# Down weights by output columns, both layers ending in PSUM, and 19 first places for expert weights

## The reference

```python
def grouped_moe(h, router_w, router_bias, w_gate, w_up, w_down):
    ...                                # each token: 1 of 4 groups, then the top 2 of its 4 experts
    a = jnp.einsum('td,edf->etf', t, w_gate)
    u = jnp.einsum('td,edf->etf', t, w_up)
    hidden = jax.nn.silu(a) * u * gates.T.astype(t.dtype)[..., None]
    out = jnp.einsum('etf,efd->td', hidden, w_down)
...
for l in range(DEPTH):
    mix = hybrid_mixer(x, w_in[l], attn_sinks[l], conv_w[l], a_log[l], dt_bias[l],
                       dn_norm_w[l], w_out[l], cos, sin)
    x = layer_norm(ALPHA * x + mix, ln1_g[l], ln1_b[l])
    ffn = grouped_moe(x, router_w, router_bias, w_gate[l], w_up[l], w_down[l])
    x = layer_norm(ALPHA * x + ffn, ln2_g[l], ln2_b[l])
```

## Time and profile before

| | us |
|---|---|
| median of three runs | 1999.3 |
| the profiled execution | 1998.46 |
| its span, first to last instruction | 1996.7 |
| PE busy | 1921.4 |
| DVE busy | 686.5 |
| ACT busy | 329.5 |
| DMA queue q1, share of 16 engines | 69.0% |

### The profile page before, as it was taken

How to read it: one execution, slowest core, us unless ns; L and a number is a source line. 1 busy time by engine, 2 the same in 40 slices (tenths; PEclk the granted TensorE clock), 3 DMA queues, 4 the chain that set the end, 5 groups by cost and what they waited for, 6 DMA issues and landing times.

```text
span 1996.7 us, 27957 instructions
## 1 busy us (share of the span) xinstructions
PE 1921.4 (96%) x11409; PEld 1194.3 (60%) x11409; DVE 686.5 (34%) x1385; ACT 329.5 (17%) x616; POOL 103.0 (5%) x174
## 2 busy tenths in 40 slices
PE   8999999999999999999899999999999999999996
PEld 7888886666644434444488888766665444443443
DVE  5444434553501111111483434445534011111104
ACT  1104220110311110111211231111103111110112
POOL 4000030012000000000000001200210000000000
PEclk9999999999999999999999999999999999999998
DMA  7433342228699999999934434422397999999995
GB/s 243 148 127 127 127 148 86 85 64 321 271 408 422 422 422 422 422 422 422 406 112 146 139 112 147 135 75 68 103 368 275 411 421 422 422 422 422 422 421 243
DMA packets 128842, 539.16 MB, mean 270 GB/s; under 512 B 15856, under 2 KB 20464, under 8 KB 78320
## 3 DMA queue, kind: packets, MB, share of 16 engines
q1 hardware_dynamic: 128752, 537.86, 69.0%
HBM read 535.73 MB, written 2.10 MB: 269 GB/s over the span
## 4 chain that ended last, share of the span: by engine, by line
PE 68%; DMA 25%; DVE 5%; issue 1%; ACT 0%; SPq 0%; DVEq 0%; ACTq 0%
PE bank L860 17%; DMA ring<-in_w_down_dram 13%; DMA ring<-in_w_up_dram 12%; PE bank L1405 10%; PE bank L871 9%; PE bank L919 8%; PE bank L1453 6%; PE bank L1190 3%; PE bank L953 3%; PE bank L1337 3%; PE bank L787 1%; DMA x_t<-in_w_up_dram 1%; PE bank L1066 1%; PE bank L1349 0%; PE bank L1161 0%
## 5 line engine op out<-in xcount | busy, mean ns | idle before, releaser
L860 PE MATMUL bank<-x_t,ring 128*128 128x256 f32 x1536 | 342.6, 382 | 0.0
L860 PEld LDWEIGHTS bank<-x_t,ring 128*128 128x128 f32 x1536 | 288.4, 190 | 48.8 <-issue 11.2
L2333 DVE TENSOR_TENSOR region_a<-bank,region_a 128x512 f32<-128x512 f32 x16 | 11.1, 692 | 566.3 <-PE bank L1405 566.3
L1405 PE MATMUL bank<-ring,region_a 128*64 128x512 f32 x704 | 159.6, 596 | 13.1 <-DMA ring<-in_w_up_dram 13.1
L1337 PEld LDWEIGHTS bank<-prob_t,x_nat 128*128 128x128 f32 x1024 | 115.5, 192 | 12.0 <-issue 11.4
L871 PE MATMUL bank<-ring,mix_acc 128*128 128x512 f32 x256 | 121.3, 604 | 1.4 <-ACT mix_acc L1663 1.4
L1453 PE MATMUL bank<-ring,region_a 128*64 128x512 f32 x512 | 115.1, 594 | 5.9 <-DMA ring<-in_w_down_dram 5.8
L1337 PE MATMUL bank<-prob_t,x_nat 128*128 128x128 f32 x1024 | 118.6, 277 | 0.0
L1405 PEld LDWEIGHTS bank<-ring,region_a 128*64 128x64 f32 x704 | 51.6, 137 | 109.3 <-issue 107.6
L1453 PE MATMUL bank<-region_b,region_a 128*64 128x512 f32 x384 | 113.3, 596 | 1.7 <-ACT region_a L1710 1.7
L2346 DVE SCALAR_TENSOR_TENSOR y_lo<-bank,slot_gate,y_hi 128x512 fp32r<-128x512 f32 x64 | 48.0, 750 | 193.1 <-ACT y_hi L1722 187.9
(11 more groups left out here) (424 smaller groups left out, 2413.0 us busy)
## 6 DMA issues: line engine op xcount, KB each, us to landing
ring<-in_w_up_dram SPq DMA_DIRECT2D x88, 1024.0 KB, 19.5
ring<-in_w_in_dram SPq DMA_DIRECT2D x80, 1024.0 KB, 5.0
ring<-in_w_down_dram SPq DMA_DIRECT2D x64, 1024.0 KB, 23.4
region_b<-in_w_gate_dram SPq DMA_DIRECT2D x48, 1024.0 KB, 19.6
region_b<-in_w_down_dram SPq DMA_DIRECT2D x48, 1024.0 KB, 20.6
ring<-in_w_gate_dram SPq DMA_DIRECT2D x36, 1024.0 KB, 22.4
ring<-in_w_out_dram SPq DMA_DIRECT2D x32, 1024.0 KB, 5.2
x_t<-in_w_up_dram SPq DMA_DIRECT2D x32, 1024.0 KB, 19.1
```

Of the source, the lines that this page charges most:

```text
L860: m = pe.matmul(b[c // 2][:, (c % 2) * T:(c % 2 + 1) * T], w[:, kk, c * P:(c + 1) * P], xT[:, k, :], start=(k == 0 and c % 2 == 0), stop=( ...
L1405: m = pe.matmul(bank[2 + w][rows, :], xg_half[k // 8][:, k % 8 * P + rows.start:k % 8 * P + rows.stop], weights(n + e)[:, kk * PANEL:(kk + ...
```

## The change

It has five parts.

1. **Down pieces by output columns.** A down piece is now all four f (512 rows) of one panel of 512 output columns: 4 rows of 2 KB for each partition. PE runs over the panels outside and over f inside, in the order 1, 2, 3, 0, and signals `down_done` after each panel.
2. **19 first places.** Three places are added (`region_cd` twice, `rot_slot` once, a new tile that holds what was `v_rot`, `k_rot` and `k_t`); with the 12 they make 15, which the first two pairs go round through. Four more are used once (`mix_acc` twice, `region_a` twice). The first 19 issues are n = 0 to 18 of the first pair. The third pair on goes by the 12 again. The second pair is written out apart (`turn=1`).
3. **`acc` later.** `mix_acc` holds weights at first, so ACT copies alpha x into `acc` after the first pair's up products; the routing's scratch moves to `region_a`, and ACT waits for `route_ready` in the first pair.
4. **Both layers end in PSUM.** In the last pair of either layer, PE puts `acc` of tile 0 into banks 0 to 3 after the first panel, and `column_out` adds one panel of the scatter (and tile 1's residual) after each further panel. DVE takes statistics panel by panel; ACT normalises from PSUM.
5. **The last LayerNorm is divided.** Five panels go to DVE in two passes, three to ACT and POOL; five stores in place of four. To fit, the mixer's panels use other banks.

```diff
-    FIRST = 4
-    PAIR_COUNTED = PAIR_PIECES - 2
+    EXTRA_SLOTS, FIRST = 3, 4
+    LEAD = EXP_SLOTS + EXTRA_SLOTS
+    LEAD_SLOTS = list(range(1, EXP_SLOTS + EXTRA_SLOTS)) + [0]
+    FIRST_ONCE = (12, 13, 14, 15)
+    LEAD_ORDER = [g for g in range(2 * PAIR_PIECES) if g not in FIRST_ONCE]
+    LEAD_HOME = {g: LEAD_SLOTS[i % LEAD] for i, g in enumerate(LEAD_ORDER)}
+    LEAD_HOME.update({g: LEAD + i for i, g in enumerate(FIRST_ONCE)})
+    PAIR_COUNTED = 16
...
-                    src = w_down_v[bass.ds(le, 1), :, (n - 16) // 2, :].rearrange("a p d -> (a p) d")
+                    c = DOWN_ORDER[(n - 16) // 2]
+                    src = w_down_v[bass.ds(le, 1), :, :, c * PANEL:(c + 1) * PANEL].rearrange("a p f d -> (a p) f d")
                 dst, arrived = home
+                if n >= 16:
+                    dst = dst.rearrange("p (f d) -> p f d", f=FC)
                 sp.dma_start(dst, src).then_inc(arrived.sem, 16)
...
+            def lead_piece(g, counted, ended, l):
+                pair, n = g // PAIR_PIECES, g % PAIR_PIECES
+                user = lead_before(g)[-1]
+                user_pair, user_n = user // PAIR_PIECES, user % PAIR_PIECES
+                if user_n < PAIR_COUNTED:
+                    sp.wait_ge(ring_free.sem, counted + (EXP_SLOTS + user_pair * PAIR_COUNTED + user_n + 1))
+                else:
+                    sp.wait_ge(down_done.sem, ended * 4 + (user_pair * 4 + (user_n - 16) // 2 + 1))
...
-                        for m in ((), (0, 1), (), (2, 3, 12, 13))[j]:
-                            expert_piece(m, early, first_home(m))
+                        for m in ((), (0, 1), (), (2, 3, 11, 16, 17))[j]:
+                            expert_piece(m, early, lead_home(m))
...
+                def column_out(q, m):
+                    c = DOWN_ORDER[m]
+                    cols = slice(c * PANEL, (c + 1) * PANEL)
+                    pe.wait_ge(y_ready.sem, (q + (l + 1)) * 4 + (m + 1))
+                    for t in range(NT):
+                        if t:
+                            residual(1, c)
+                        pe.matmul(bank[4 * t + c][:, :], scat[:, t, :], y_hi[:, cols], start=False, stop=False)
+                        pe.matmul(bank[4 * t + c][:, :], scat[:, t, :], y_lo[:, cols], start=False, stop=True)\
+                            .then_inc(scat_put.sem, 1)
...
-                    for f in range(FC):
-                        n = 16 + 2 * f
-                        if last and l == depth - 1 and f == 2:
+                    for m, c in enumerate(DOWN_ORDER):
+                        n = 16 + 2 * m
+                        if last and m == 1:
                             pe.wait_ge(scat_ready.sem, q + (l + 2))
                             pe.wait_ge(scat_added.sem, scat_added.at(q + l, 8))
-                            for c in range(4):
-                                residual(0, c)
+                            for cc in range(4):
+                                residual(0, cc)
...
+                        for f in range(FC):
                             for e in range(2):
                                 rows = slice(e * SLOTS, (e + 1) * SLOTS)
-                                m = pe.matmul(bank[4 + c][rows, :], hid_t[:, f, rows],
-                                              weights(n + e)[:, c * PANEL:(c + 1) * PANEL],
-                                              start=(f == 0), stop=(f == FC - 1))
+                                mm = pe.matmul(bank[4 + c][rows, :], hid_t[:, f, rows],
+                                               weights(n + e)[:, f * PANEL:(f + 1) * PANEL],
+                                               start=(f == 0), stop=(f == FC - 1))
+                        mm.then_inc(down_done.sem, 1)
+                        if last and m:
+                            column_out(q, m - 1)
+                    if last:
+                        column_out(q, 3)
+                        return
```

More of the change, by code:

```diff
@@ L152, in trunk @@
     PAIR_PIECES = 24
-    FIRST = 4
-    PAIR_COUNTED = PAIR_PIECES - 2
-    assert MIX_PIECES % RING == 0 and PAIR_PIECES == 2 * EXP_SLOTS and PAIR_COUNTED == 22
+    EXTRA_SLOTS, FIRST = 3, 4
[5 more added lines that the diff above has]
+    LEAD_HOME.update({g: LEAD + i for i, g in enumerate(FIRST_ONCE)})
+    LEAD_USES = [sum(home == s for home in LEAD_HOME.values()) for s in range(LEAD)]
+    assert all(uses == 3 for uses in LEAD_USES[1:]) and LEAD_USES[0] == 2
+    PAIR_COUNTED = 16
+    assert MIX_PIECES % RING == 0 and PAIR_PIECES == 2 * EXP_SLOTS
     MIX_USES = MIX_PIECES // RING
@@ L380, in trunk @@
         fast_read = signal("fast_read", 3 * N_FAST)
+        extra_landed = [signal(f"extra_landed{i}", 3) for i in range(EXTRA_SLOTS)]
         first_landed = [signal(f"first_landed{i}", 1) for i in range(FIRST)]
@@ L629, in _ @@
                         combine(l, f, j)
+            pool.wait_ge(affine_loaded.sem, affine_loaded.at(depth - 1, 32))
+            for i, (t, c) in enumerate(POOL_FINAL):
+                part = x_nat[:, t, c * PANEL:(c + 1) * PANEL]
+                g, b = (ln_par[:, w, c * PANEL:(c + 1) * PANEL] for w in range(2))
+                pool.wait_ge(final_norm.sem, i + 1)
+                pool.tensor_tensor(part, part, g, ALU.mult).then_inc(final_pool.sem, 1)
+                pool.wait_ge(final_pool.sem, i + 1)
+                pool.tensor_tensor(part, part, b, ALU.add).then_inc(final_added.sem, 1)
         @block.sync
@@ L1688, in _ @@
                 act.sem_inc(y_ready.sem, 4)
-                for t in range(NT):
-                    m = act.activation(acc[:, t, :].rearrange("p (q c) -> p q c", c=KC),
-                                       x_nat[:, t, :].rearrange("p (c q) -> p q c", c=KC), ACT.Copy, scale=ALPHA)
-                m.then_inc(acc_ready.sem, 1)
                 pairs0 = pairs1 if l else 0
@@ L1717, in pair_turn @@
                     act.activation(scat_rows[:, :], bank[0][:, 0:NT * P], ACT.Copy).then_inc(scat_ready.sem, 1)
+                    if first:
+                        act.wait_ge(gateup_done.sem, q * 2 + 2)
+                        for t in range(NT):
+                            m = act.activation(acc[:, t, :].rearrange("p (q c) -> p q c", c=KC),
+                                               x_nat[:, t, :].rearrange("p (c q) -> p q c", c=KC), ACT.Copy, scale=ALPHA)
+                        m.then_inc(acc_ready.sem, 1)
                     act.wait_ge(scat_ready.sem, q + (l + 2))
```

299 lines of the change are left out of this document (157 added, 142 removed).

## The result

The changed kernel takes **2007.4 us** (median of 6 runs, 2006.8 to 2008.1), the kernel before 1999.0 (6 runs): ratio 1.0042, 95% interval 1.0029 to 1.0055. It is slower by 8.4 us. The forecast was 2009.5 us, and slower with a chance of 0.69. The profiled execution has a span of 2006.4 us against 1996.7, +9.7; the forecast sum was +10.8.

The account below looks back on a forecast made before the run. DMA bytes at 422 GB/s bound the expert stage from each layer's fourth pair on. Profiled 1998.46 us +4.5 (layer 1 stage) +3.3 (boundary) +4.5 (layer 2 stage) -1.5 (tail) = 2009.3, stated as 2009.5; range 1995 to 2017.

Parts of the forecast that it names:

- T in layer 1: Expert stage: the time TensorE takes up the last up pieces, 960.50 us before, moves by +4.5 us to 965.
- The lead: Expert stage start: 19 first places leave three pieces fewer behind 537 us, -7.5 us in each layer.
- the hole at the third pair's start: Expert stage, where 12 places are left: possible 1 us of idle DMA, offset near 580 us, counted at nothing.
- The rows: Expert stage: 53 down pieces in 2 KB rows, each 0.225 us slower, +11.9 us in each layer.
- One sign: Before the first gate products: no idle DMA between 520 and 532 us, some between 532 and 538.
- Rate: Expert stage: 2 KB rows at 387 GB/s, 2.71 us a piece; late pairs 61.4 us, stage 408 to 411 GB/s.
- the mixer's single pieces: Rival of a draw: 2 KB pieces at up to 403 GB/s with a shallow queue, 2.60 us each; 1997.8 us, chance 0.13.
- End of layer 1: Boundary to layer 2: column-wise scatter, residual products and normalising from PSUM cost +3.3 us, bounds 0 to +6.
- the residual products' time: End of layer 1, TensorE: four new residual products take 3.63 us that nothing hides, as TensorE isn't waiting there.
- End of layer 2: Tail: span ends 38.1 us after the last pair's down products start, 39.6 before; -1.5 us, bounds -3 to +1.
- Starvation: Rival, SP's queue: down issues hold SP until engines run dry 2 us a pair, +28 us, 2037 us; chance 0.08.
- The lead wins: Rival, expert stage: 2 KB rows cost little, 2.49 to 2.58 us a piece; 1985.3 to about 1994.5 us; chance 0.17.

Follow-up runs that it names:

- k2: Changed kernel with down weights in the old order again (8 KB rows, products by rows); first places and both PSUM ends stay: 1987.4 us, ratio 0.9944.
- e3: Kernel before, with each down piece read as 512 rows of 2 KB in place of 128 rows of 8 KB: 2020.6 us, ratio 1.0113.
- k3: Changed kernel with 8 KB down rows in the old order and the old end of layer 1 with its fillers: 1983.6 us, ratio 0.9926.
- e5: Kernel before without the 14 filler products among TensorE's scatter products at the end of layer 1: 1999.7 us, ratio 1.0008.
- e1: Changed kernel with each down piece read as 128 rows of 8 KB in place of 512 of 2 KB, wrong columns: 1987.3 us, ratio 0.9947.

## Why the prediction was right

*T in layer 1.* Forecast 965 (+4.5), measured 963.83 (+3.3); counted from the gate products +3.8, and +3.4 in layer 2. Both terms were too large, in opposite directions, so a part of the closeness is luck. The lead was put at -7.5 a layer; with 8 KB rows it gives -5.9 and -7.2 (k2 against before), as the hole at the third pair's start is real, and with 2 KB rows -7.4 and -6.6 (changed kernel against e3). The prediction had seen that hole and counted it at nothing. The rows were put at +11.9; they cost 9.8 and 10.6 (changed kernel against k2). One sign wasn't met: the DMA engines were to have no idle time between 520 and 532, and their share there is 0.73. The 19 pieces had landed by 530.7 us without a full queue to the end; what counts, three pieces fewer behind 537 us, held.

*Rate.* The 2.71 us a piece were taken from two windows of 387 GB/s, and give 61.4 us a pair and 408 to 411 GB/s; the trace has 61.42 us and 409. Holding to these windows rather than to the mixer's single pieces (2.60) was right. Between 8 and 2 KB rows the runs have 2.485 and 2.71 us, 9%. The Trainium skill's "DMA: Bandwidth & Descriptors", section "Why small descriptors are slow (HBM only)", would make it 3.5% by its 3 cycles a packet; the runs don't agree, and the measurement decides.

*End of layer 1.* Forecast +3.3, measured +4.0 (37.2 - 33.2). The order of the steps was right, their lengths a little short. A column of down products was put at 3.4 us and takes 3.58 (972.67 to 976.25), so TensorE ends the scatter at S + 25.8 in place of 24.8. ScalarE starts tile 0 at S + 26.9 in place of 26.1 and tile 1 at S + 33.1 in place of 32.7, and from there to the long run pass 4.1 us (3.35 before, 3.75 by the forecast). The new end by itself costs 3.4 with fast rows (k2 against k3). The prediction had called the residual products' time uncovered by DMA, which holds for this kernel, but with the old end TensorE would have waited 2.3 us for slow pieces; undoing it would return only 2.0. The removed fillers, which the prediction missed, cost 0.1 to 0.3 us of it (e5 against before, changed kernel against e1), too little for single traces to tell from nothing, although the clock fell as deep as 0.50.

*End of layer 2.* Forecast S + 38.1, measured 38.6, -1.0 in place of -1.5. With 8 KB rows it is 38.0 to 38.1. GpSimd is the end, as the bound had it: six passes of 1.26 us, paced by 1.3, that start at 1995.42 = S + 27.6 in place of 27.1:

```profile
1995.42 1.26 POOL L656 TENSOR_TENSOR x_nat<-x_nat,region_cd 128x512 f32<-128x512 f32 x1 [528.59 <-ACT x_nat L1794]
...
2001.90 1.26 POOL L658 TENSOR_TENSOR x_nat<-x_nat,region_cd 128x512 f32<-128x512 f32 x1
```

*Rivals.* Starvation (2037) was decided where the prediction put it. SyncE does stand, for 0.4 to 8.5 us at a down issue of layer 1, and for some 26 us in each late pair:

```profile
823.30 24.54 SPq L703 DMA_DIRECT2D ring<-in_w_down_dram  x6
848.01 2.45 SPq L703 DMA_DIRECT2D x_t<-in_w_down_dram  x1
```

But the last of these lands 14.2 us after its issue begins, so 12 us of transfers still lie ahead when SyncE is free again. "The lead wins" describes e1, k2 and k3 and not this kernel. The sum: +10.8, less 1.2 and 1.1 for T (+3.3 and +3.4 for 4.5), plus 0.7 at the boundary, plus 0.5 at the tail, makes 9.7, as measured. Nothing is left for the mixer, which was counted at nothing: from the long run to layer 2's first gate product pass 1527.40 - 1009.79 = 517.6 us, before 517.6.

## What to carry to other kernels

Once a stage is bound by bytes, the row size of its largest streams is a first-order cost: ask of every change of layout how many bytes one descriptor covers, and put that beside what the new order gains; here a lead worth 13 to 15 us was bundled with a layout that cost 20. Measure the parts of such a bundle one by one, since the best kernel was neither the one before nor the changed one. And where bytes arrive faster but no sooner, look at when the last of the 16 parts of a transfer lands, not at the mean rate.

## What the runs showed of the hardware

- Full queue, piece of 1.0486 MB: 2.485 us with 8 KB rows, 2.56 with 4 KB, 2.71 with 2 KB, 3.01 with 1 KB, from the time between late pairs (59.63, 60.23, 61.42, 63.86 us). That is 9 to 10 ns a row on each engine beside its bytes, at every step.
- 4 KB rows in place of 2 KB shortened a late pair by 1.2 us and raised the time between the first and last of a transfer's 16 completions from 2.2 to 8.0 us; the time of the kernel did not change.
- SyncE is held at the issues of pieces with many rows: 2.45 us at the late ones of a pair with 512 rows (8.5 at the longest in layer 1), 2.79 with 1024, 2.31 with 256, and 0.33 to 0.76 as a rule with 128. It cost nothing, since DMA's share stayed at 1.02 to 1.05.
- After an idle stretch of 2.6 us TensorE's granted clock was 0.50 (1.2 GHz) for some 3 us in most kernels with the new end and 1.00 throughout in e1, with the same idle time; in e1 the next long run came 0.3 us earlier, in one trace each.
